# Gated delta rule in a streaming encoder: the powers and the inverse of the 16-token blocks kept as packed 32-column tiles

## The chip, the cores and the metric

The kernel runs on one core of one Trainium2 chip. The metric is the device time of one execution in microseconds. The engines are TensorE (PE), VectorE (DVE), ScalarE (ACT), GpSimd (POOL) and SyncE (SP); they run side by side and wait for each other by semaphores only.

## What is computed

A two-layer encoder trunk over 256 tokens of width 2048, all in float32: a gated DeltaNet layer, then an S5 layer, each with its MLP and an input embedding. The change lies in the DeltaNet layer. It has 32 value heads and 16 key heads of 128, and it is computed in chunks of 64 tokens:

```python
m = jnp.where(strict, jnp.einsum('bhnid,bhnjd->bhnij', kb, k) * decay, 0.0)
t_inv = lax.linalg.triangular_solve(eye + m, jnp.broadcast_to(eye, m.shape),
                                    left_side=True, lower=True, unit_diagonal=True)
u = jnp.einsum('bhnij,bhnjd->bhnid', t_inv, v * beta[..., None])
w = jnp.einsum('bhnij,bhnjd->bhnid', t_inv, kb * jnp.exp(gc)[..., None])
...
v_new = u_n - jnp.einsum('bhck,bhkv->bhcv', w_n, state)
```

What matters here is t_inv, the inverse of a unit lower triangular 64x64 matrix for each chunk and head.

## The kernel before

Every large product streams its weights from HBM in chunks of 2048x128 numbers. ACT rounds a chunk to w_hi (L280), DVE computes the rest w_lo = raw - w_hi (L286), in four quarters of 128x512 each, and PE multiplies a quarter by four key tiles (L299 to L303). One order of the work is written out by hand for each engine; nothing is scheduled by a planner.

The DeltaNet layer has 16 rounds (`head(r)` on PE, ACT and DVE), one for each key head with its two value heads. A round has 24 steps. In each step PE multiplies one quarter of the streamed projection weights, which belong to the next heads, and then does one part of the delta rule (`core(r, s)`), so that the products fill the time in which a part waits for ACT and DVE. ACT and DVE have the same two kinds of work in their queues: the splits of the weights (`low(s)` on DVE) and the parts.

The four matrices of a round (two value heads, two blocks of 128 tokens, so two chunks on the diagonal of each) lie side by side as [128, 4, 128] in one tile. The inverse is built from the inside. `key_matrix` (L1796) forms Mp, the matrix m, and keeps in Pm minus its part within blocks of 16 tokens. The inverse of such a block is (I + P)(I + P^2)(I + P^4)(I + P^8). RT holds the transposed inverse so far, starting as P^T + I (L1811). DVE's transpose turns blocks of 32x32 on the spot, which turns these block-diagonal matrices completely. The steps of the change are:

- step 0: PE squares P into bank C (`four`, L633, four products of 128x128 with 128 columns each), ACT copies it to P2.
- step 1: PE multiplies P2 by RT into bank A; DVE adds it to RT (`add_to_R`, L1838). DVE turns P2 into P2T (L1842), PE multiplies P2T by P2 for the fourth power, ACT copies it to P4.
- step 2: the same with P4 and P4T (L1847), giving P8; PE also does the products of q and k (L656).
- step 3: PE multiplies P8 by RT, DVE adds; PE turns k (L663).
- steps 4 to 9: the blocks of 16 are joined to 32, 64 and the chunk, with products of Mp, RT and Dm, the transpose of RT (L667 to L701). The first, L667, waits for the third `add_to_R`.

The order of DVE's queue around it is fixed in `head`: after `key_matrix(r + 1)` come mid_lo (L1922), `low(22)`, `low(23)`, and in the next round `low(0)`, the transpose of P2, `low(1)`, the first addition, `low(2)`, the transpose of P4, a convolution (`conv`, L1769 to L1775), the second addition, the masked products of q and k with `low(3)` between them (L1854, L1857), the third addition, and the transpose of RT (L1860). P2, P8, WT and the output tile oy share the tile T[0]; therefore ACT waits for mid_lo of the round before in step 0.

## Time and profile before

| | |
|---|---|
| median of 3 runs | 3187.47 us (3186.65 to 3192.27) |
| span of the profiled execution | 3188.2 us (its own run time is not listed apart from the three) |
| PE busy | 3099.4 us, 97% |
| DVE busy | 2246.8 us, 70% |
| ACT busy | 1742.8 us, 55% |
| POOL busy | 821.5 us, 26% |
| HBM traffic | 556.43 MB, 175 GB/s over the span |

The 16 rounds of the DeltaNet layer lie between about 87 and 899 us of the span; the rest is the output projection, the MLPs and the S5 layer. Busy times of the engines overlap. A line number points to the instruction's source line, and for helpers (L286 is `split_lo`, L941 is ACT's `A_`) to the helper. Matmuls are pipelined: an instruction's end lies later than the start of the next.

### The profile page before, as it was taken

What the parts mean: (1) busy time and instruction counts of PE and PEld (TensorE: products, weight loads), DVE (VectorE), ACT (ScalarE), POOL (GpSimd) and SP (SyncE); (2) the same over time, 40 slices, a digit from 0 to 9 for tenths busy, and PEclk for the clock granted to TensorE, in tenths of its full rate; (3) what the DMA queues carried; (4) which work ended last, traced back from release to release, by engine and by line L of the source; (5) the groups of instructions that cost most, each with busy time, mean ns of one, the idle gap of its engine ahead of it and who ended that gap; (6) DMA issues with size and microseconds to landing.
All of it is one profiled execution on the core that took longest, in us unless ns stands there. A gap on an engine that the chain in (4) does not pass through costs nothing.

```text
span 3188.2 us, 63691 instructions
## 1 busy us (share of the span) xinstructions
PE 3099.4 (97%) x19926; PEld 2737.0 (86%) x19926; DVE 2246.8 (70%) x4157; ACT 1742.8 (55%) x3855; POOL 821.5 (26%) x1372
## 2 busy tenths in 40 slices
PE   5999999999999999999999999999999999999998
PEld 4999999999978888888888887888888888888887
DVE  5767777777755788667887767886677654776566
ACT  5565666566644555445555556764555544555444
POOL 1000000000010499888888810770000000000000
PEclk8999999999999999999999999999999999999999
DMA  6454444444467777877777766785666677667764
GB/s 166 115 135 123 125 122 132 128 125 122 132 170 190 195 204 208 226 203 203 202 206 208 211 183 166 231 247 153 185 182 186 189 185 185 183 185 185 185 159 142
DMA packets 1036179, 556.43 MB, mean 175 GB/s; under 512 B 38193, under 2 KB 1023953, under 8 KB 1035585
## 3 DMA queue, kind: packets, MB, share of 16 engines
q1 hardware_dynamic: 969088, 491.18, 57.8%
q10 hardware_dynamic: 58160, 37.63, 4.0%
q0 software_dynamic: 8848, 26.59, 2.7%
q8 instruction: 44, 0.72, 0.1%
q14 instruction: 39, 0.31, 0.0%
HBM read 528.30 MB, written 27.03 MB: 174 GB/s over the span
## 4 chain that ended last, share of the span: by engine, by line
PE 73%; DVE 11%; ACT 7%; issue 6%; DMA 1%; ACTq 1%; DVEq 0%; POOL 0%; SPq 0%; POOLq 0%
PE bank L302 39%; PE bank L303 21%; DVE w_lo L286 5%; ACT w_hi L280 3%; PE bank L633 2%; PE bank L299 1%; ACT T L941 1%; PE bank L300 1%; DVE tiles L1935 1%; ACT L941 1%; DVE normed L1947 1%; DVE tiles L328 1%; PE bank L798 1%; ACT dec L941 1%; DVE y L1775 1%
## 5 line engine op out<-in xcount | busy, mean ns | idle before, releaser
L286 DVE TENSOR_TENSOR w_lo<-raw,w_hi 128x512 fp32r<-128x512 f32 x1856 | 1298.1, 752 | 145.2 <-ACT w_hi L280 137.3
L302 PE MATMUL bank<-act,w_hi 128*128 128x512 f32 x3376 | 1227.5, 405 | 17.5 <-DVE w_lo L286 7.8
L303 PE MATMUL bank<-act,w_lo 128*128 128x256 f32 x4352 | 1224.3, 281 | 0.0
L302 PE MATMUL bank<-mid,w_hi 128*128 128x512 f32 x3072 | 1088.1, 399 | 4.1 <-DVE w_lo L286 3.1
L280 ACT ACTIVATE w_hi<-raw 128x512 fp32r<-128x512 f32 x1856 | 1040.9, 620 | 68.7 <-PE bank L303 44.1
L303 PE MATMUL bank<-mid,w_lo 128*128 128x256 f32 x3072 | 860.7, 280 | 0.0
L303 PEld LDWEIGHTS bank<-act,w_lo 128*128 128x128 f32 x4352 | 827.9, 190 | 0.8
L302 PEld LDWEIGHTS bank<-act,w_hi 128*128 128x128 f32 x3376 | 638.1, 189 | 171.9 <-DVE w_lo L286 11.2
L302 PEld LDWEIGHTS bank<-mid,w_hi 128*128 128x128 f32 x3072 | 579.1, 188 | 147.0 <-issue 3.4
L303 PEld LDWEIGHTS bank<-mid,w_lo 128*128 128x128 f32 x3072 | 581.6, 189 | 0.2 <-issue 0.2
L318 ACT ACTIVATE tiles<-bank 128x256 f32<-128x256 f32 x323 | 123.5, 382 | 541.8 <-PE bank L303 535.6
L328 DVE TENSOR_TENSOR tiles<-bank,tiles 128x256 f32<-128x256 f32 x288 | 121.4, 421 | 357.0 <-ACT tiles L318 349.3
L299 PE MATMUL bank<-act,w_hi 128*128 128x256 f32 x976 | 296.1, 303 | 0.0
L300 PE MATMUL bank<-act,w_hi 128*128 128x256 f32 x976 | 276.1, 283 | 0.0
L1436 POOL DMA_DIRECT2D chunk_no<-in_constants_dram x1 | 0.5, 548 | 828.4 <-DVE mid L1922 828.4
L299 PEld LDWEIGHTS bank<-act,w_hi 128*128 128x128 f32 x976 | 186.8, 191 | 5.5 <-issue 3.6
L300 PEld LDWEIGHTS bank<-act,w_hi 128*128 128x128 f32 x976 | 187.2, 192 | 4.5 <-issue 4.1
L941 ACT ACTIVATE mid<-normed 128x256 f32 (+1 forms) x128 | 53.5, 418 | 247.6 <-DVE normed L1947 247.6
L941 ACT ACTIVATE T<-bank 128x512 f32<-128x512 f32 (+2 forms) x144 | 68.8, 478 | 204.2 <-PE bank L633 75.4
L1949 DVE TENSOR_TENSOR mid<-normed,mid 128x256 f32 (+1 forms) x128 | 59.1, 462 | 94.3 <-ACT mid L941 94.3
L338 ACT ACTIVATE sqb<-h 128x256 f32 (+1 forms) x96 | 40.1, 418 | 130.6 <-DVE h L1979 62.3
L1775 DVE SCALAR_TENSOR_TENSOR y<-pre,conv_f,y 128x256 f32<-128x256 f32 x192 | 93.1, 485 | 6.8
(331 smaller groups left out, 3122.6 us busy)
## 6 DMA issues: line engine op xcount, KB each, us to landing
raw<-in_mlp_w_up_dram SPq DMA_DIRECT2D x128, 1024.0 KB, 6.6
raw<-in_mlp_w_down_dram SPq DMA_DIRECT2D x128, 1024.0 KB, 6.2
raw<-in_gdn_w_in_dram SPq DMA_DIRECT2D x96, 1024.0 KB, 6.0
raw<-in_gdn_w_out_dram SPq DMA_DIRECT2D x32, 1024.0 KB, 6.8
raw<-in_ple_w_gate_dram SPq DMA_DIRECT2D x32, 1024.0 KB, 6.3
raw<-in_s_w_out_dram SPq DMA_DIRECT2D x28, 1024.0 KB, 6.8
raw<-in_s_w_in_dram ACTq DMA_DIRECT2D x10, 1024.0 KB, 7.1
c_scratch<-c_pow ACTq DMA_DIRECT2D x32, 256.0 KB, 4.6
```

The lines of the kernel that those rows point to most:

```text
L280: eng.activation(w_hi[par][:, c], raw[slot][:, c], ACT.Copy).then_inc(S("hi_ready"), 1)
L286: eng.tensor_tensor(w_lo[par][:, c], raw[slot][:, c], w_hi[par][:, c].bitcast(F32), ALU.subtract).then_inc(S("lo_ready"), 1)
L299: eng.matmul(a[:, 0:NT], w_hi[par][:, w], rhs[:, k0 + kt, 0:NT], start=(k0 + kt == 0), stop=False)
L300: eng.matmul(a[:, 0:NT], w_hi[par][:, w], rhs[:, k0 + kt, NT:2 * NT], start=False, stop=False)
L302: eng.matmul(a[:, :], w_hi[par][:, w], rhs[:, k0 + kt, :], start=(k0 + kt == 0), stop=False)
L303: mm = eng.matmul(a[:, 0:NT], w_lo[par][:, w], rhs[:, k0 + kt, 0:NT], start=False, stop=(k0 + kt == kend - 1))
L318: eng.activation(half[:, par, :], acc[par][:, NT:2 * NT], ACT.Copy).then_inc(S("half_copied"), 1)
L328: eng.tensor_tensor(dst, acc[par][:, 0:NT], half[:, par, :], ALU.add).then_inc(S("acc_freed"), 1)
L633: mm = pe.matmul(bk[:, m * P:(m + 1) * P], lhs[:, m, :], rhs[:, m, :], start=True, stop=True)
L941: return se.activation(dst, src, f, **kw)
L1775: ins = STT(y[:, j, :], pre[:, j, k:k + NT], conv_f[:, j, k:k + 1], y[:, j, :], ALU.mult, ALU.add)
L1949: TT(mid[:, span(i * 4 + j, 1), NT:2 * NT], normed[:, a, :], mid[:, span(i * 4 + j, 1), 0:NT].bitcast(F32), ALU.subtract).then_inc(S("hidd ...
```

## The change

The diagonal blocks of 32x32 hold all that is not zero, so four matrices of 128x128 fit into 32 columns each. The new tile pr is [128, 4, 2, 32]: for each matrix the packed transposed power (index 0) and the packed transposed inverse (index 1). Two tiles px[0], px[1] hold the power spread out again as a block-diagonal 128x128 matrix, as a stationary operand; their other blocks are cleared once at the start by POOL. `four` multiplies px (in step 0 Pm itself) by 32 or 64 columns of pr: with 64 the one product gives the next power and the inverse's update together. Step 0 has 32 columns, steps 1 and 2 have 64, step 3 has 32.

On DVE, `key_matrix` turns Pm by four transposes, one for each 32 partitions, into pr, and adds a packed identity. `spread(i, src)` writes the four blocks of a power into px by four transposes; the first two read ACT's copy, the third reads bank C directly. `add_to_R` works on the packed halves. The convolution comes after the third spread and the second addition. The last update of the inverse is written into RT, block by block, by four additions.

RT's other blocks must be zero now when they are read (ACT fills some of them later in a round, as before), so POOL clears three regions of RT in each round once the key products are done, and DVE's last additions wait for that (`RT_cleared`). ACT makes two copies of 128x128 instead of three of 128x512, and its wait for mid_lo moves from step 0 to step 4, since only WT is left in T[0] there.

```diff
@@ -158,16 +158,22 @@
         gcr = gs("gcr", [P, 4, P])
+        pr = gs("pr", [P, 4, 2, 32])
+        px = [gs(f"px{i}", [P, 4, P]) for i in range(2)]
+        ident32 = gs("ident32", [P, 32])
         g1.close()
+
+        block_32 = lambda t_, j: t_[32 * j:32 * j + 32, :, 32 * j:32 * j + 32]
+        pair_of = lambda bk, i: bk[:, 0:256].rearrange("p (m i q) -> p m i q", m=4, i=2)[:, :, i, :]
...
-        P2, P8, WT, osq, oy = (T[0],) * 5
-        rn, Pm, P4, Dm = (T[1],) * 4
-        sq, PT, P4T = (T[2],) * 3
-        P2T, VN, orn = (T[3],) * 3
+        WT, osq, oy = (T[0],) * 3
+        rn, Pm, Dm = (T[1],) * 3
+        sq = T[2]
+        VN, orn = (T[3],) * 2
@@ -625,12 +631,10 @@
-            def four(bk, lhs, rhs, name, turn_=False):
+            def four(bk, power, first, count, name):
                 for m in range(4):
-                    if turn_:
-                        mm = pe.transpose(bk[:, m * P:(m + 1) * P], lhs[:, m, :], ident)
-                    else:
-                        mm = pe.matmul(bk[:, m * P:(m + 1) * P], lhs[:, m, :], rhs[:, m, :], start=True, stop=True)
+                    mm = pe.matmul(bk[:, m * 64:m * 64 + 32 * count], power[:, m, :],
+                                   pr[:, m, first:first + count, :].rearrange("p i q -> p (i q)"), start=True, stop=True)
                 mm.then_inc(S(name), 1)
@@ -638,27 +642,25 @@
                     w("PT_ready")
-                    four(C, PT, Pm, "power_done")
+                    four(C, Pm, 0, 1, "power_done")
                 elif s == 1:
-                    w("power_out", 3, 1)
                     w("RT_ready", 7, 1)
-                    four(A, P2, RT, "R_done")
-                    w("transposed_out", 2, 1)
-                    four(C, P2T, P2, "power_done")
+                    w("power_out", 2, 1)
+                    w("spread_out", 3, 1)
+                    four(A, px[0], 0, 2, "power_done")
                 elif s == 2:
-                    w("power_out", 3, 2)
                     w("RT_ready", 7, 2)
-                    four(A, P4, RT, "R_done")
-                    w("transposed_out", 2, 2)
-                    four(C, P4T, P4, "power_done")
+                    w("power_out", 2, 2)
+                    w("spread_out", 3, 2)
+                    four(C, px[1], 0, 2, "power_done")
                     w("o_normed")
...
                 elif s == 3:
-                    w("power_out", 3, 3)
                     w("RT_ready", 7, 3)
-                    four(A, P8, RT, "R_done")
+                    w("spread_out", 3, 3)
+                    four(A, px[0], 1, 1, "R_done")
                     w("o_log")
@@ -1081,25 +1083,23 @@
                 if s == 0:
-                    w("mid_lo")
+                    w("RT_ready", 7, 1)
                     w("power_done", 3, 1)
-                    A_(fl(P2), C[:, :]).then_inc(S("power_out"), 1)
+                    A_(pr[:, :, 0, :], pair_of(C, 0)).then_inc(S("power_out"), 1)
                 elif s == 1:
                     w("power_done", 3, 2)
-                    A_(fl(P4), C[:, :]).then_inc(S("power_out"), 1)
-                elif s == 2:
-                    w("power_done", 3, 3)
-                    A_(fl(P8), C[:, :]).then_inc(S("power_out"), 1)
+                    A_(pr[:, :, 0, :], pair_of(A, 0)).then_inc(S("power_out"), 1)
                 elif s == 3:
...
                 elif s == 4:
+                    w("mid_lo")
                     w("X_done", 3, 1)
...
                 elif s == 5:
-                    w("R_done", 6, 4)
+                    w("R_done", 4, 2)
                     for j in range(4):
@@ -1107,7 +1107,7 @@
                 elif s == 7:
-                    w("R_done", 6, 5)
+                    w("R_done", 4, 3)
                     for j in range(2):
@@ -1119,7 +1119,7 @@
                 elif s == 9:
-                    w("R_done", 6, 6)
+                    w("R_done", 4, 4)
                     A_(RT[0:64, :, 64:128], C[0:64, 0:256].rearrange("p (m q) -> p m q", m=4), scale=-1.0).then_inc(S("RT_ready"), 1)
@@ -1425,11 +1425,20 @@
                 gp.dma_start(dst, src, allow_slow_non_contiguous=dst.shape[-1] == 1).then_inc(S("side_in"), 16)
+            for t_ in px:
+                gp.memset(t_[:, :, :].rearrange("p m q -> p (m q)"), 0.0).then_inc(S("px_cleared"), 1)
+            gp.memset(RT[:, :, :].rearrange("p m q -> p (m q)"), 0.0).then_inc(S("RT_cleared"), 1)
             gp.wait_ge(S("gc_turned_out"), 1)
...
             gp.dma_start(gcr[:, :, :].rearrange("p (b h) q -> p b (h q)", b=2), gc_rows(0)).then_inc(S("gc_saved"), 16)
+            with gp.Fori(1, KH) as r:
+                gp.wait_ge(S("kk_done"), r + 1)
+                gp.sem_inc(S("RT_read"), 1)
+                gp.memset(RT[0:32, :, 32:64], 0.0).then_inc(S("RT_cleared"), 1)
+                gp.memset(RT[64:96, :, 96:128], 0.0).then_inc(S("RT_cleared"), 1)
+                gp.memset(RT[0:64, :, 64:128], 0.0).then_inc(S("RT_cleared"), 1)
             gp.wait_ge(S("t_in"), 16)
@@ -1749,6 +1758,7 @@
             link(ve.memset(pre[:, :, 0:4], 0.0))
+            link(ve.memset(WT[96:128, :, :].rearrange("p m q -> p (m q)"), 0.0))
@@ -1806,10 +1816,17 @@
                 ve.wait_ge(S("P_ready"), r + 1)
-                ve.transpose(fl(PT), fl(Pm)).then_inc(S("PT_ready"), 1)
+                for j in range(4):
+                    last = ve.transpose(pr[32 * j:32 * j + 32, :, 0, :], block_32(Pm, j))
+                last.then_inc(S("PT_ready"), 1)
                 ve.wait_ge(S("PT_ready"), r + 1)
-                TT(RT[:, :, :], PT[:, :, :], ident.unsqueeze(1).to_broadcast([P, 4, P]), ALU.add).then_inc(S("RT_ready"), 1)
-
+                TT(pr[:, :, 1, :], pr[:, :, 0, :], ident32[:, :].unsqueeze(1).to_broadcast([P, 4, 32]),
+                   ALU.add).then_inc(S("RT_ready"), 1)
+
+            link(TT(ident32[:, :], ident[:, 0:32], ident[:, 32:64], ALU.add))
+            link(TT(ident32[:, :], ident32[:, :], ident[:, 64:96], ALU.add))
+            link(TT(ident32[:, :], ident32[:, :], ident[:, 96:128], ALU.add))
+            ve.wait_ge(S("px_cleared"), 2)
             scalars(0)
@@ -1832,21 +1849,28 @@
-                def add_to_R(i):
-                    w("R_done", 6, i)
+                def spread(i, src):
+                    if i < 3:
+                        w("power_out", 2, i)
+                    else:
+                        w("power_done", 3, 3)
+                    for j in range(4):
+                        last = ve.transpose(block_32(px[(i + 1) % 2], j), src[32 * j:32 * j + 32])
+                    last.then_inc(S("spread_out"), 1)
+
+                def add_to_R(i, bk):
                     w("RT_ready", 7, i)
-                    TT(fl(RT), A[:, :], fl(RT), ALU.add).then_inc(S("RT_ready"), 1)
+                    TT(pr[:, :, 1, :], pair_of(bk, 1), pr[:, :, 1, :], ALU.add).then_inc(S("RT_ready"), 1)
                 low(0)
-                w("power_out", 3, 1)
-                ve.transpose(fl(P2T), fl(P2)).then_inc(S("transposed_out"), 1)
+                spread(1, pr[:, :, 0, :])
                 low(1)
-                add_to_R(1)
+                spread(2, pr[:, :, 0, :])
+                add_to_R(1, A)
                 low(2)
-                w("power_out", 3, 2)
-                ve.transpose(fl(P4T), fl(P4)).then_inc(S("transposed_out"), 1)
+                spread(3, pair_of(C, 0))
+                add_to_R(2, C)
                 conv(r, n + 2, 2)
-                add_to_R(2)
@@ -1855,7 +1879,12 @@
                 TT(qkT[:, :, :], qkT[:, :, :], U.unsqueeze(1).to_broadcast([P, 4, P]), ALU.mult).then_inc(S("qkT_ready"), 1)
-                add_to_R(3)
+                w("R_done", 4, 1)
+                w("RT_ready", 7, 3)
+                w("RT_cleared", 3, 1)
+                for j in range(4):
+                    whole = TT(block_32(RT, j), pair_of(A, 0)[32 * j:32 * j + 32], pr[32 * j:32 * j + 32, :, 1, :], ALU.add)
+                whole.then_inc(S("RT_ready"), 1)
                 w("RT_ready", 7, 4)
```

On DVE, at the start of a round's part (transposes and additions between the weights' splits). Before, up to the first addition to the inverse:

```order
L1842 STREAM_TRANSPOSE T<-T 128x512 [waits power_out]
L284 REGISTER_ALU
L286 TENSOR_TENSOR w_lo<-raw,w_hi 128x512 [waits hi_ready]
L1829 REGISTER_ALU
L1829 ISA [waits R_done]
L1838 TENSOR_TENSOR RT<-bank,RT 128x512 [waits RT_ready]
L284 REGISTER_ALU
L286 TENSOR_TENSOR w_lo<-raw,w_hi 128x512 [waits hi_ready]
```

Now, from the first spread on; px is the spread-out power, pr the packed tile:

```order
L1858 STREAM_TRANSPOSE px<-pr 32x4x32 [waits power_out]
L1858 STREAM_TRANSPOSE px<-pr 32x4x32 x3
L290 REGISTER_ALU
L292 TENSOR_TENSOR w_lo<-raw,w_hi 128x512 [waits hi_ready]
L1846 REGISTER_ALU
L1858 STREAM_TRANSPOSE px<-pr 32x4x32 [waits power_out]
L1858 STREAM_TRANSPOSE px<-pr 32x4x32 x3
L1846 ISA
L1863 TENSOR_TENSOR pr<-bank,pr 128x4x32 [waits RT_ready]
L290 REGISTER_ALU
L292 TENSOR_TENSOR w_lo<-raw,w_hi 128x512 [waits hi_ready]
```

The one transpose of the whole tile became four of 32 partitions, the second spread comes ahead of the first addition, and between the two spreads lies one split.

On DVE, in front of the first product that joins blocks (L667). Before, from the product of q and k to the transpose of RT:

```order
L1854 TENSOR_TENSOR qkT<-dec,bank 128x512 [waits qk_done]
L284 REGISTER_ALU
L286 TENSOR_TENSOR w_lo<-raw,w_hi 128x512 [waits hi_ready]
L1857 TENSOR_TENSOR qkT<-qkT,masks 128x512 [waits qk_decay]
L1829 REGISTER_ALU [waits R_done]
L1838 TENSOR_TENSOR RT<-bank,RT 128x512 [waits RT_ready]
L1829 REGISTER_ALU
L1860 STREAM_TRANSPOSE T<-RT 128x512 [waits RT_ready]
```

Now:

```order
L1878 TENSOR_TENSOR qkT<-dec,bank 128x512 [waits qk_done]
L290 REGISTER_ALU
L292 TENSOR_TENSOR w_lo<-raw,w_hi 128x512 [waits hi_ready]
L1881 TENSOR_TENSOR qkT<-qkT,masks 128x512 [waits qk_decay]
L1846 REGISTER_ALU
L1846 REGISTER_ALU [waits R_done]
L1846 REGISTER_ALU [waits RT_ready]
L1886 TENSOR_TENSOR RT<-bank,pr 32x4x32 [waits RT_cleared]
L1886 TENSOR_TENSOR RT<-bank,pr 32x4x32 x3
L1846 REGISTER_ALU
```

The last addition is four instructions, with a wait for POOL's clears. The convolution, which stood between the second transpose and the second addition, now stands between the second addition and this place.

## Rows read from the trace of the kernel before

**Rows 1.** Page, first part: busy time, share of the span, instructions.
```profile
PE 3099.4 (97%) x19926; PEld 2737.0 (86%) x19926; DVE 2246.8 (70%) x4157; ACT 1742.8 (55%) x3855; POOL 821.5 (26%) x1372
```

**Rows 2.** Windows, one round; columns: us, busy of each engine (instructions), PEclk, DMA.
```profile
433.36:485.13 51.77, 51.25 (x397) 47.71 (x397) 38.38 (x78) 32.70 (x74) 0.00 (x0) 1.00 0.48 127
```

**Rows 3.** Waits of PE, rounds between 122.72 and 847.49: waiter, releaser, total, times, longest.
```profile
PE bank L633 <- DVE T L1842: 3.3, 14, 0.2
PE bank L633 <- DVE T L1809: 2.7, 14, 0.2
```

**Rows 4.** Chain of waits through one round: start us, us, what.
```profile
433.36 1.17 ACT dec L941 x4
...
442.56 0.69 DVE qkn L1793
...
452.17 1.16 PE bank L633 x8
...
476.16 0.46 PE bank L712 x4
```

**Rows 5.** Timeline of DVE in that round: start us, us, instruction, [idle before <-releaser].
```profile
447.64 0.71 DVE L1809 STREAM_TRANSPOSE T<-T 128x512 f32<-128x512 f32 x1
448.39 0.69 DVE L1811 TENSOR_TENSOR RT<-T,consts 128x512 f32<-128x512 f32 x1
449.00 0.69 DVE L1922 TENSOR_TENSOR mid<-T,mid 128x512 f32 x1
449.60 1.89 DVE L286 TENSOR_TENSOR w_lo<-raw,w_hi 128x512 fp32r<-128x512 f32 x3
451.41 0.71 DVE L1842 STREAM_TRANSPOSE T<-T 128x512 f32<-128x512 f32 x1
...
454.63 0.13 DVE L1769 COPY conv_f<-conv_w 128x4 f32 x1
...
456.62 0.68 DVE L1838 TENSOR_TENSOR RT<-bank,RT 128x512 f32<-128x512 f32 x1
457.22 0.68 DVE L1854 TENSOR_TENSOR qkT<-dec,bank 128x512 f32<-128x512 f32 x1
...
459.38 0.69 DVE L1838 TENSOR_TENSOR RT<-bank,RT 128x512 f32<-128x512 f32 x1 [0.28 <-PE bank L633]
...
461.65 0.42 DVE L328 TENSOR_TENSOR z<-bank,tiles 128x256 f32<-128x256 f32 x1
461.98 0.41 DVE L1781 SCALAR_TENSOR_TENSOR y<-tiles,y 128x256 f32<-128x256 f32 x1
```

**Rows 6.** Timeline of PE in the same stretch.
```profile
448.50 1.13 PE L633 MATMUL bank<-T 128*128 128x128 f32 x8 [0.20 <-DVE T L1809]
...
450.88 1.05 PE L633 MATMUL bank<-RT,T 128*128 128x128 f32 x8
452.17 1.16 PE L633 MATMUL bank<-T 128*128 128x128 f32 x8 [0.23 <-DVE T L1842]
...
454.58 1.05 PE L633 MATMUL bank<-RT,T 128*128 128x128 f32 x8
455.47 1.06 PE L633 MATMUL bank<-T 128*128 128x128 f32 x8
...
460.60 0.91 PE L667 MATMUL bank<-RT,Mp 128*112 128x64 f32 x8
```

**Rows 7.** Timeline of DVE, its only small transpose of the round.
```profile
468.56 0.30 DVE L1876 STREAM_TRANSPOSE T<-RT 32x128 f32<-32x128 f32 x1 [1.05 <-ACT RT L941]
```

**Rows 8.** Timeline of ACT: two runs of four instructions, two copies out of PSUM.
```profile
433.26 1.27 ACT L941 ACTIVATE dec<-gcr,hs 128x128 f32<-128x128 f32 x4
...
453.36 0.60 ACT L941 ACTIVATE T<-bank 128x512 f32<-128x512 f32 x1 [2.44 <-PE bank L633]
...
463.76 0.89 ACT L941 ACTIVATE RT<-bank 16x64 f32<-16x64 f32 x4 [1.31 <-PE bank L673]
...
476.64 0.38 ACT L941 ACTIVATE state<-bank 128x256 f32<-128x256 f32 x1 [0.66 <-PE bank L712]
```

## The prediction

> **What bounds the kernel now.** I read the page first. TensorE (PE) is busy for 97% of the span [rows 1], so the change, which takes matmul columns away, seems to aim at the right engine. But a busy PE says nothing about one stage, so I went to the stage that the change touches, the rounds of the delta rule. They repeat exactly: a round takes 51.77 us, with PE busy for 51.25, VectorE (DVE) for 38.38, ScalarE (ACT) for 32.70, GpSimd (POOL) for nothing, at a granted clock of 1.00 [rows 2]. Next the waits of PE over the 14 middle rounds: only two sorts, both of 0.2 us a round, and both at the very products of the change, for DVE's transposes at L1809 and L1842 [rows 3]. That is the warning. The chain of waits says why: in a round it runs over ACT at 433.36, over DVE from 442.56, over PE only from 452.17 to 476.16, and then over ACT and DVE again [rows 4]. A round is thus a ring that is PE's for half its length. The first powers lie on the DVE half, and PE looks full there because it multiplies streamed weights while DVE works.
>
> The DVE instructions of this half follow each other without a gap: 447.64, 448.39, 449.00, 449.60 (three w_lo tiles), 451.41 [rows 5]. PE starts its second power at 452.17, when the transpose of 451.41 (0.71 long) ends, and did the inverse's product at 450.88 while it waited [rows 5, 6].
>
> **What the change does to PE.** Six groups of four products of 128 columns become four groups of 32 or 64 columns. A group now costs 0.89 (454.58 to 455.47) [rows 6]. The nearest row to the new ones, four products of 64 columns with 112-wide weights, starts at 460.60 and lasts 0.91 against 1.05 for a 128-column group [rows 6]. So a new group ends about 0.95 after it starts and holds PE for some 0.79; from nothing saved (0.89) to columns alone (0.22 for 32 columns) are the ends. I take 0.79: PE's own work falls by 6 x 0.89 - 4 x 0.79 = 2.2 us a round. That is worth something only where PE ends last.
>
> **What it does to DVE.** One transpose of 128x512 becomes four of 32x128, each on another 32 partitions, and that four times a round (the first power, three spreads) where there were three. The last addition becomes four instructions too. Three additions shrink to 128x128. The prices:
> - A small transpose: the only one in the trace lasts 0.30 alone [rows 7]. A 128x512 one lasts 0.71, and fills the four groups of partitions at once [rows 5]. Two ends for four small ones: if each waits for the one before, 4 x 0.30 = 1.20; if they overlap as whole-width neighbours do (128x512 additions last 0.68 and start every 0.60, 128x256 ones last 0.42 and start every 0.33 [rows 5], so 128 elements start every 0.20), 3 x 0.20 + 0.30 = 0.90. The floor is one whole transpose, 0.71.
> - Which end? ACT does both kinds in this round. Four 128x128 instructions on all partitions take 1.27 together, though one lasts 0.39 on average, so they overlap. Four of 16x64, each on other partitions, take 0.89, and one lasts 0.215: four times 0.215 is 0.86, so nothing overlaps [rows 8]. I take the first end, 1.20, for DVE too. The Trainium skill says this of DVE itself (VectorE: DVE Perf Modes, the section on two Vector instructions with no wait between them): an instruction that starts in another group of 32 partitions than the last one is held until every earlier one has finished. By that rule the group is 1.20. No DVE row here has such neighbours, so no row confirms it.
> - A small addition lasts 0.29 (0.42 less half of 0.68 - 0.42): four on different partitions 1.16, or 0.89 if they overlap. On all partitions a 128x128 one takes 0.20 instead of 0.60.
>
> **The new path**, on the clock of this round, from the first transpose at 447.64:
> 1. Four transposes into the packed tile, 1.20 and 0.04 to the next: 448.88 (before 448.39). The identity's addition 0.20 for 0.61; mid 0.60, three w_lo 1.80: DVE is free at 451.48 (before 451.41). The copy of the packed power was ready long before: PE from about 449, 0.95, and a 128x128 copy of 0.27 on ACT (0.60 for 512 elements, 0.38 for 256 [rows 8]).
> 2. Spread 1, 1.20: PE's next group starts at 452.73. PE has been ready since 448.95 + 0.79 + 1.49 (a quarter, 448.50 to 450.88 less 0.89 [rows 6]) = 451.2. The inverse's product that filled this hole is merged into the late one: 1.5 us of PE lie open.
> 3. The merged product after a stall: 1.0; copy 0.27 and 0.06 of handing over; spread 2 from 454.06 to 455.26. The next merged product reads the inverse's half too, so it also waits for the first packed addition, 0.29 behind the spread: PE at 455.60 (its old pair began at 454.58). DVE was free from 453.3 on, after one w_lo: a new wait of 0.7.
> 4. Product 1.0; DVE does a w_lo meanwhile; spread 3 reads the bank from 456.63 to 457.83.
> 5. Only now comes the convolution, which used to start at 454.63: addition 0.20, convolution 1.99 (454.63 to 456.62), masked q k 0.60, w_lo 0.60, mask 0.60 (456.62 to 457.22 is one such step) [rows 5]: 461.82. Before, DVE had these behind it early enough to start the last addition at 459.38, after a wait of 0.28 for PE.
> 6. Four final additions 1.16 and handing over 0.06: PE starts L667 at 463.05 instead of 460.60 [rows 6].
>
> So PE, which had saved 2.2 us of work, stands still for 2.5 us in front of L667 (from its second pair at 455.47 to L667 it now takes 5.13, two groups included [rows 6]; 455.60 + 5.13 - 2 x 0.10 = 460.5), and the round is longer by **2.45 us**. From L667 to 476.16 PE ends last as before: DVE is later than PE by another half microsecond there, but had waits of its own. Nothing later is shortened, since the rest of the ring is untouched. The part is run once per pair of heads, 16 times: 16 x 2.45 = 39.2 us.
>
> **Costed at nothing.** ACT's three copies shrink by 0.3 each and lose the third; ACT waits for PE in front of them, and stands on the ring elsewhere. ACT's wait for mid_lo moves to a place four steps later, long after the signal. Its tanh is queued behind the convolution, 3 us later than now, and the four instructions behind the tanh, the copy of L667's result last, are ACT steps of at most 0.60 each: from 460.0 they are through by about 462, before L667 even starts, so that copy is not late. POOL's three clears are released by the key products, 15 us before the additions need them, and POOL is empty; if they got in DVE's way, I put it at one small instruction, 0.30 a round. The opening's four extra DVE instructions (about 1 us) lie in front of a stretch where DVE waits for ACT's w_hi; without that cover they cost 1 us once.
>
> The profiled span is 3188.2 us, 0.7 above the median of 3187.47; no time of its own is given for that execution, so I put the sum on the median: 3187.5 + 39.2 = **3227 us**.
>
> **The rivals.**
> - **Small instructions overlap**, 0.90 and 0.89 a group. Five groups lie on the path, so 2.45 - 4 x 0.30 - 0.27 = 1.0 a round: 3203. Speaks for it: DVE's whole-width neighbours overlap. Against: ACT's do not across partitions. The Trainium skill (Vector Engine (DVE) Microarchitecture Reference, measured stream behaviour) gives some 75 ns per instruction beside 1.04 ns per element; that makes an estimated 0.21 each, 0.83 a group, near this case.
> - **A group costs no more than the whole transpose did**, 0.71, by four groups of partitions at work together: 2.45 - 5 x 0.47 = 0.1 a round, 3189, no change. No row shows two DVE instructions in full overlap.
> - **PE ends last after all, and the kernel is faster.** With no stall PE would go from 448.50 to L667 in 12.1 - 6 x 0.89 - 0.4 of stalls + 4 x 0.79 = 9.5 us, 2.6 less: 16 x 2.6 = 42, 3146. The place is the queue between 451.41 and 459.38. It decides only if DVE has its final additions done by 458.0, which is 5.0 us sooner than my path; even the overlapping case finds only 1.5 of them. Partial gains lie between.
> - **More than I count**: a gap behind each held instruction (0.05 x 20 = 1 us a round, 3243), or a clock that falls. Before, PE never stands for more than 0.2 us in a round and the clock is 1.00; now it would stand for 1.5 and 2.5. If it fell to the lower level for one quarter, about 1.4 us more a round: 3249.
>
> **How the numbers follow.** Forecast 0.60, overlap 0.15, no change 0.08, faster 0.08, more than counted 0.09. The likeliest gives 3227. Leaving out the two cases below and the far end of the last one, the range is 3196 to 3246. A measurement of this kernel can tell about 0.2%, 6.4 us. Slower by more than that: 0.60 + 0.09 and most of the overlap case, 0.82; within it 0.09; faster 0.09.
>
> **What would show it.** In the profile after: rounds of about 54.2 us; PE waiting some 1.5 us a round at its second power group for the DVE spread, and over 2 us at the successor of L667 for the final additions; four transposes in about 1.2; the convolution more than 3 us later in the round; PE busy share lower, with no drop of the clock. I am wrong in the price if four small ones take 0.9, and wrong in the mechanism if PE waits nowhere between the first power and that product, or if the round is shorter than 51.6.

## The result, and the profile after

The changed kernel takes 3248.9 us (median of 4 runs, 3241.98 to 3263.9), the kernel before in the same comparison 3187.99 us. The ratio is 1.0201, with a 95% interval of 1.0172 to 1.023: the change costs 2%, 61 us. The forecast had the direction (slower, 0.82) and the place; its 3227 us is 22 us short, and the time lies 2.9 us above the range. The profiled execution is the slowest of the four, 3263.9 us with a span of 3262.2.

The page, parts 1 and 5 (busy time, share of the span, instructions; and GpSimd's new row):

```profile
PE 3097.8 (95%) x19670; PEld 2719.3 (83%) x19670; DVE 2287.7 (70%) x4417; ACT 1721.9 (53%) x3839; POOL 822.6 (25%) x1420
...
L1439 POOL MEMSET RT<- 32x128 f32 x15 | 2.9, 194 | 840.4 <-PE bank L608 840.4
```

TensorE's busy time fell by 1.6 us in all [rows 1], although 256 matmul instructions are gone. DVE has 260 instructions more and 41 us more work. The clears by POOL are 0.19 us each and nobody waits for them.

The rounds are measured between DVE's first instructions on Mp. The windows of the first round, of a stretch of the second, and of two neighbouring rounds in the middle; columns: us, busy of each engine (instructions), PEclk, DMA share, GB/s:

```profile
83.62:141.90 58.28, 53.27 (x371) 48.78 (x370) 39.21 (x91) 29.79 (x69) 0.70 (x3) 0.91 0.42 116
159.90:168.00 8.10, 8.04 (x39) 7.43 (x39) 6.11 (x14) 2.70 (x8) 0.00 (x0) 0.59 0.44 121
423.34:479.98 56.64, 51.60 (x381) 47.13 (x380) 40.90 (x95) 31.46 (x73) 0.70 (x3) 0.97 0.44 116
479.98:535.10 55.12, 50.06 (x381) 45.75 (x380) 40.67 (x95) 31.47 (x73) 0.70 (x3) 1.00 0.45 119
```

Two things lie here on top of each other. A round at a granted clock of 1.00 takes 55.08 us on average against 51.77 [rows 2], 3.31 more. PE's busy time in it fell by 1.2 us while the round grew by 3.3, so PE now stands still for 5 us of each. And six of the 15 rounds are longer still: the first three at 58.1 to 58.3 us with a clock of 0.91 to 0.94, and three later ones at 56.65 with 0.97. In the stretch at 0.59 the engine ran mostly at the lower of its two levels, 1.2 GHz; it had stood for 2.24 us just before.

The waits of PE, 14 rounds between 132 and 920 us:

```profile
PE bank L669 <- DVE RT L1886: 31.4, 14, 2.2
PE bank L636 <- DVE px L1858: 17.9, 14, 1.3
PE bank L636 <- DVE pr L1820: 10.4, 14, 0.7
PE bank L636 <- DVE pr L1863: 9.7, 14, 0.7
```

Where there were two waits of 0.2 us a round [rows 3] there are four, of 2.2, 1.3, 0.7 and 0.7 us, together 5.0 us (69.4 / 14), and all are for DVE. The chain of waits through the same half of a round at clock 1.00 (start us, us, what) runs on DVE, with PE as short steps in between, where before it was PE's from the second power on [rows 4]:

```profile
538.38 1.06 PE bank L636 x8
...
541.82 0.32 DVE px L1858
542.18 1.12 PE bank L636 x8
...
544.91 0.30 DVE pr L1863
545.43 1.11 PE bank L636 x8
...
550.12 0.68 DVE qkT L1878
551.32 0.69 DVE qkT L1881
552.81 0.31 DVE RT L1886
553.16 1.00 PE bank L669 x8
```

DVE's timeline of this stretch answers to [rows 5]; columns: start, us, instruction, and in brackets the idle time before it with its releaser:

```profile
536.98 1.25 DVE L1820 STREAM_TRANSPOSE pr<-T 32x128 f32<-32x128 f32 x4
538.26 0.29 DVE L1823 TENSOR_TENSOR pr<-pr,ident 128x128 f32<-128x128 f32 x1
...
540.88 1.24 DVE L1858 STREAM_TRANSPOSE px<-pr 32x128 f32<-32x128 f32 x4
542.15 0.69 DVE L292 TENSOR_TENSOR w_lo<-raw,w_hi 128x512 fp32r<-128x512 f32 x1
543.63 1.25 DVE L1858 STREAM_TRANSPOSE px<-pr 32x128 f32<-32x128 f32 x4 [0.78 <-ACT pr L943]
544.91 0.29 DVE L1863 TENSOR_TENSOR pr<-bank,pr 128x128 f32<-128x128 f32 x1
545.12 0.68 DVE L292 TENSOR_TENSOR w_lo<-raw,w_hi 128x512 fp32r<-128x512 f32 x1
546.57 1.29 DVE L1858 STREAM_TRANSPOSE px<-bank 32x128 f32<-32x128 f32 x4 [0.76 <-PE bank L636]
...
551.92 1.18 DVE L1886 TENSOR_TENSOR RT<-bank,pr 32x128 f32<-32x128 f32 x4
```

A group of four transposes lasts 1.25 us, 0.31 for each, where one whole transpose lasted 0.71; the four last additions last 1.18. The group holds DVE for 1.27 us (540.88 to 542.15). A whole transpose, ahead of an instruction that does not wait for it, held DVE for 0.62 us, from 451.41 [rows 5] to this line of the kernel before:

```profile
452.03 0.65 DVE L286 TENSOR_TENSOR w_lo<-raw,w_hi 128x512 fp32r<-128x512 f32 x1
```

DVE also idles twice now, 0.78 us for ACT's copy and 0.76 for PE's bank, because DVE, PE and ACT hand one small result round in a ring.

PE's timeline in the same stretch:

```profile
539.26 0.48 PE L308 MATMUL bank<-act,w_hi 128*128 128x512 f32 x1
...
542.18 1.10 PE L636 MATMUL bank<-pr,px 128*128 128x64 f32 x8 [1.28 <-DVE px L1858]
543.09 0.48 PE L308 MATMUL bank<-act,w_hi 128*128 128x512 f32 x1
...
545.43 1.10 PE L636 MATMUL bank<-pr,px 128*128 128x64 f32 x8 [0.68 <-DVE pr L1863]
...
553.16 1.00 PE L669 MATMUL bank<-RT,Mp 128*112 128x64 f32 x8 [2.24 <-DVE RT L1886]
```

The timeline of the weight loads (PEld), after:

```profile
542.18 0.97 PEld L636 LDWEIGHTS bank<-pr,px 128*128 128x128 f32 x8 [1.60 <-DVE px L1858]
```

The same view of the kernel before:

```profile
454.46 0.97 PEld L633 LDWEIGHTS bank<-RT,T 128*128 128x128 f32 x8
...
460.48 0.88 PEld L667 LDWEIGHTS bank<-RT,Mp 128*112 128x112 f32 x8
```

And PE's next instruction behind that L667 group, in the kernel before:

```profile
461.31 0.48 PE L302 MATMUL bank<-act,w_hi 128*128 128x512 f32 x1
```

The groups with 32 columns begin at 538.38 and 548.31 and the next instruction of PE at 539.26 and 549.22: 0.88 and 0.91. A group with 64 columns takes 542.18 to 543.09, 0.91. With 128 columns it was 0.89 [rows 6]. The number of columns makes no difference from 32 to 128, and the eight weight loads of a group take 0.97 us either way. What does count is how wide the weights are. The L667 group has 64 columns too, but weights of 112 columns instead of 128: its loads take 0.88 us, and PE goes on 0.71 us after its start (460.60 [rows 6] to 461.31). The Trainium skill (TensorE: Matmul & The Clock Gate, the section on LDWEIGHTS) has that rule: the load goes by the columns of the stationary operand. Its figure of columns / 1.2 ns gives an estimated 8 x 107 ns = 0.85 us for a group, and the 0.88 to 0.91 us from a group to the next instruction agree within 0.06.

### The profile page after: what moved, and what is told of

Same layout as the page of the kernel before. It is cut to its first block, busy times and chain, and to the rows that moved or that the text cites. A ratio compares the mean times of both kernels' runs of the same rounds, so it can differ in the third digit from the quotient of the medians.

```text
span 3262.2 us, 63592 instructions
## 1 busy us (share of the span) xinstructions
PE 3097.8 (95%) x19670; PEld 2719.3 (83%) x19670; DVE 2287.7 (70%) x4417; ACT 1721.9 (53%) x3839; POOL 822.6 (25%) x1420
## 4 chain that ended last, share of the span: by engine, by line
PE 65%; DVE 16%; ACT 9%; issue 7%; DMA 2%; ACTq 1%; DVEq 1%; POOL 0%; SPq 0%; POOLq 0%
PE bank L308 35%; PE bank L309 19%; DVE w_lo L292 5%; ACT w_hi L286 3%; PE bank L636 2%; DVE px L1858 1%; PE bank L305 1%; ACT T L943 1%; PE bank L306 1%; DVE y L1785 1%; DVE tiles L334 1%; DVE tiles L1964 1%; DVE normed L1976 1%; ACT L943 1%; ACT uf L943 1%
## 5 line engine op out<-in xcount | busy, mean ns | idle before, releaser
L308 PE MATMUL bank<-act,w_hi 128*128 128x512 f32 x3376 | 1235.7, 408 | 20.1 <-DVE w_lo L292 8.8
L308 PE MATMUL bank<-mid,w_hi 128*128 128x512 f32 x3072 | 1091.1, 400 | 5.5 <-DVE w_lo L292 4.5
L308 PEld LDWEIGHTS bank<-act,w_hi 128*128 128x128 f32 x3376 | 643.3, 191 | 175.4 <-DVE w_lo L292 14.3
L308 PEld LDWEIGHTS bank<-mid,w_hi 128*128 128x128 f32 x3072 | 578.8, 188 | 150.3 <-DVE w_lo L292 4.1
L943 ACT ACTIVATE T<-bank 112x256 f32<-112x256 f32 (+2 forms) x96 | 40.1, 417 | 128.8 <-PE bank L726 44.9
```

The lines of the kernel that those rows point to most:

```text
L308: eng.matmul(a[:, :], w_hi[par][:, w], rhs[:, k0 + kt, :], start=(k0 + kt == 0), stop=False)
L943: return se.activation(dst, src, f, **kw)
```

## The experiments

Theory: the end of this half of a round is set by DVE's queue, made longer by (a) four instructions for one, (b) a convolution of 2 us in front of the last update, and (c) the handing round between engines; on top of it the stall of 2.24 us ahead of L669 lets the clock fall in some rounds. Rivals: the cost lies in the new waits themselves wherever DVE's work stands; small instructions are dear by their number and not by their partitions; the clock has nothing to do with the stall. Each comparison has its own runs of the kernel before: e1 to e4 one chip (before: 3186.62 us), e5 to e8 another (3186.21), the last four a third (3187.33).

**e1_conv_early**: the convolution back in front of the third spread.

```diff
                 low(2)
+                conv(r, n + 2, 2)
                 spread(3, pair_of(C, 0))
                 add_to_R(2, C)
-                conv(r, n + 2, 2)
```

> Only the order on DVE is changed: the convolution goes back in front of the third spread, where DVE waits 0.76 us a round for PE. Theory A (DVE's queue sets the end of the round's first half, and PE waits for its last additions): the 0.76 us are filled, PE waits 0.8 us less in front of the first joining product, an undisturbed round takes 54.3 us instead of 55.1, and the time falls by 12 us, to about 3237. Theory B (the chain power, copy, spread, product sets it): the third spread and the fourth product group come over 1 us later, and the round takes 55.5 us or more.

3233.21 us (3221.57 to 3239.03, 4 runs), ratio 1.0146 (1.0109 to 1.0182). Rounds 54.22 us, all at clock 1.00. The wait ahead of L669 fell from 2.2 us to 0.2, but the one for the second packed addition (L1863) rose to 1.1: the convolution now holds up the third spread. So its place costs 0.86 us of the 3.31, not the 2 us that it lasts.

**e2_both_filled**: in addition `low(2)` goes ahead of the second spread, into the time in which DVE waits for ACT.

```diff
                 low(1)
+                low(2)
                 spread(2, pr[:, :, 0, :])
                 add_to_R(1, A)
-                low(2)
+                conv(r, n + 2, 2)
                 spread(3, pair_of(C, 0))
                 add_to_R(2, C)
-                conv(r, n + 2, 2)
```

> Order on DVE again: the third w_lo quarter goes in front of the second spread (DVE waits 0.78 us there) and the convolution in front of the third. Theory A: both waits are filled, nearly 1.5 us leave the path, an undisturbed round takes 53.6 us, the time is about 3225, still slower than before by 1%. Theory B: 55 us or more a round.

3220.77 us (3202.8 to 3225.4, 4 runs), ratio 1.0105 (1.0059 to 1.015), rounds 53.63 at clock 1.00, as worked out. Both orders together are worth 1.45 us a round, and 1.86 remain.

**e3_same_group**: the four transposes of a spread all read the first 32 partitions of a tile of zeros and write to the first 32 of px. Their number, size and waits stay; only the change of partitions is gone. The powers above the first so become zero and drop out of the inverse.

```diff
+        zt = gs("zt", [P, 4, 32])
...
                     for j in range(4):
-                        last = ve.transpose(block_32(px[(i + 1) % 2], j), src[32 * j:32 * j + 32])
+                        last = ve.transpose(px[(i + 1) % 2][0:32, :, 32 * j:32 * j + 32], zt[0:32])
```

> The four transposes of each spread all lie on the first 32 partitions and turn a tile of zeros, so the higher powers drop out of the inverse; the instructions have the same shape and number. If the price of four small instructions comes from changing the group of partitions, a group takes about 0.95 us instead of 1.25, and an undisturbed round 54.1 us. If it comes from the number of instructions alone, a group stays at 1.25 and a round at 55.1.

DVE's timeline in this kernel, a changing and an unchanging group:

```profile
358.62 1.25 DVE L1822 STREAM_TRANSPOSE pr<-T 32x128 f32<-32x128 f32 x4
...
362.52 0.87 DVE L1860 STREAM_TRANSPOSE px<-zt 32x128 f32<-32x128 f32 x4
```

Four transposes on one group of partitions take 0.87 us, four on changing groups 1.25, in one execution and with the same shapes. So without the change they do overlap, close to the 0.90 us that the prediction had put as its lower end. Counted to the start of an instruction that waits for none of them, it is 0.81 us (362.52 to 363.33) against 1.27 in the changed kernel and 0.62 for a whole transpose. Of the 0.65 us by which a group of four holds DVE longer than one whole transpose, 0.46 are the change of partitions and 0.19 the number. The small ones of e3 read another tile than the real ones; that this has no part in it was not tested. The Trainium skill (VectorE: DVE Perf Modes, the section on two Vector instructions with no wait between them) says that an instruction that starts in another group of 32 partitions is held until the earlier ones have finished, and this pair of rows agrees. Undisturbed rounds are 53.64 us, 1.4 less than with the real spreads (3 x 0.46 = 1.4). The whole kernel took 3237.05 us (2 runs, ratio 1.017, 1.0129 to 1.021) all the same, because nine of its 15 rounds ran at 0.97, and the first at 0.94: the stall ahead of L670 (L669 in the changed kernel) is still 1.8 us. That is a first sign for the clock.

**e4_fill**: nine products into an unused part of a bank ahead of PE's wait in step 4. They compute nothing that is read.

```diff
                 elif s == 4:
+                    for _ in range(9):
+                        pe.matmul(C[:, 2 * P:3 * P], kq[:, 1, 0, :], kq[:, 1, 0, :], start=True, stop=True)
                     w("RT_ready", 7, 4)
```

> Nine products of 128 columns whose result nobody reads are added on PE in front of its wait for the last additions, where it stands still for 2.2 us; they take 2.0 us and end before that wait does. If the rounds of 56.6 and 58.1 us come from TensorE's clock falling after that stall, every round now takes 55.1 us, the clock reads 1.00 and the time falls by 10 to 14 us although PE has more to do. If the clock has nothing to do with the stall, the time stays at 3249 with a mean clock of 0.985.

3245.96 us (3241.99 to 3248.99, 4 runs), ratio 1.0194 (1.0162 to 1.0226). Every round is 55.05 to 55.13 us at clock 1.00 (only the first at 0.97), but the median is not clearly below 3248.9. So both kernels were run again on one chip.

**a_again** and **e4_again**: the changed kernel, and the filled one, unchanged.

> The changed kernel unchanged, beside the filled one on one chip. Theory that the stall of 2.24 us ahead of the group that uses RT lets the clock fall in some rounds: about 3249 us, mean clock about 0.985 to 0.99, undisturbed rounds of 55.1 us with some of 56.6 to 58.3 us among them. Rival, that the 14 us of the first profile were a mishap of one execution: all rounds 55.1 us, clock 0.99 or more, about 3240 us.

> The nine filler products ahead of TensorE's wait again, on the chip that runs the changed kernel too. Theory of the clock: every round 55.1 us at 1.00, and 8 to 14 us less than the changed kernel in this comparison. Rival, that the clock costs nothing in most executions: the same time as the changed kernel within 3 us.

3251.95 us (3243.29 to 3259.54, 6 runs) and 3241.58 us (3233.59 to 3247.55, 6 runs); ratios 1.0218 (1.0188 to 1.0248) and 1.0186 (1.0158 to 1.0215), which overlap by a little. Windows of 600 us in the middle, the changed kernel and then the filled one:

```profile
300.00:900.00 600.00, 544.51 (x4094) 497.68 (x4093) 442.15 (x1012) 338.61 (x774) 7.75 (x33) 0.99 0.44 117
```

```profile
300.00:900.00 600.00, 566.65 (x4322) 520.24 (x4321) 444.88 (x1020) 340.48 (x786) 7.73 (x33) 1.00 0.45 119
```

In the changed kernel again five rounds of 15 ran at 0.94 to 0.97 and took 56.65 to 56.70 us, the others 55.05 to 55.13. In the filled one 14 of 15 are 55.05 to 55.11 us, all at 1.00, and the first is 53.97. Its 15 rounds sum to 824.9 us against 834.2. Work that nobody needs makes the kernel 9 us shorter in the rounds of the profiled executions and 10.4 us in the median. With the stall filled the clock stays up, so it is this stall that lets the clock fall. The rounds show it cleanly; the two ratios alone would not quite. Where the stall is at most 1.3 to 1.4 us (e1, e2) no round lost clock.

**e5_before_four**: the kernel before, with the transpose of P2 alone made of four small ones, into a cleared tile of its own.

```diff
+        P2T = gs("p2t", [P, 4, P])
...
-                ve.transpose(fl(P2T), fl(P2)).then_inc(S("transposed_out"), 1)
+                for j in range(4):
+                    last4 = ve.transpose(P2T[32 * j:32 * j + 32, :, 32 * j:32 * j + 32], P2[32 * j:32 * j + 32, :, 32 * j:32 * j + 32])
+                last4.then_inc(S("transposed_out"), 1)
```

> The kernel before, with one thing of the change: the transpose of P2 is four transposes of 32 partitions into a cleared tile of its own. It lies on the path (PE waits 0.23 us for it in every round). If four small instructions on changing groups of partitions run one after the other, they take 1.25 us for 0.71 and a round 52.3 us for 51.8, the time 3195. If they overlapped the round would grow by under 0.25 us.

3193.69 us (3189.53 to 3202.9, 8 runs), ratio 1.0031 (1.0012 to 1.0049). Rounds 52.31 us, 0.54 more. The four small transposes end 1.24 us after their start and the whole one after 0.71, so PE's product is released 0.53 us later; its wait for this transpose grew from 0.2 to 0.8. Here the half microsecond by which the transpose ends later is half a microsecond of the round.

**e6_masked**: the packed form, without small spreads. In e2's order DVE turns the packed power straight out of the bank by one instruction (32x32 blocks on all partitions) and multiplies it, repeated four times, by a mask of diagonal blocks into px. The last update is made the same way, so RT needs no clears by POOL. The two tiles px become one.

```diff
...
+                    ve.transpose(tp[:, :, :], pair_of(bk, 0)).then_inc(S("tp_ready"), 1)
+                    w("tp_ready", 3, i)
+                    by_block(px[(i + 1) % 2][:, :, :], tp[:, :, :]).then_inc(S("spread_out"), 1)
...
-                    whole = TT(block_32(RT, j), pair_of(A, 0)[32 * j:32 * j + 32], pr[32 * j:32 * j + 32, :, 1, :], ALU.add)
-                whole.then_inc(S("RT_ready"), 1)
+                TT(tp[:, :, :], pair_of(A, 0), pr[:, :, 1, :], ALU.add).then_inc(S("R_whole"), 1)
+                w("R_whole", 1, 1)
+                by_block(RT[:, :, :], tp[:, :, :]).then_inc(S("RT_ready"), 1)
```

> As both_filled, with whole-width instructions in the place of the groups of four: a spread is one transpose of the packed power straight out of the bank and one product with a block mask over 128x512, the last addition one packed addition and one such product; POOL clears nothing. Theory A: a spread takes 0.95 us instead of 1.28 and the last update 0.95 instead of 1.2, four places on the path, so an undisturbed round falls from 53.6 to about 52.4 us, the time to about 3198. Rival: the first power's latency holds the round, which stays above 53.

3200.07 us (3188.82 to 3206.34, 10 runs), ratio 1.0046 (1.0032 to 1.0061), rounds 52.33: 1.30 us a round less than e2. The mask product writes four times as much as is needed, and transpose and mask together (0.96 us, shown under e7) are cheaper than four exact instructions (1.27); and ACT's copy is no longer on the way to the spread. How the 1.30 us part between the two was not tested.

**e7_order**: e6 with DVE's queue in another order: the first spread ahead of `low(0)`, `low(2)` and `low(3)` ahead of the third with the convolution back behind it, and the two products of q and k (L1878, L1881) moved to behind `low(6)` and `low(7)`, where their result is still early enough.

```diff
-                low(0)
                 spread(1, C)
+                low(0)
                 low(1)
-                low(2)
                 spread(2, A)
-                conv(r, n + 2, 2)
+                low(2)
+                low(3)
                 spread(3, C)
+                conv(r, n + 2, 2)
...
                 gate(n + 3, 1, y[:, 3, :])
...
+                TT(bh(qkT), bh(dec), qk, ALU.mult).then_inc(S("qk_decay"), 1)
                 low(7)
...
+                TT(qkT[:, :, :], qkT[:, :, :], U.unsqueeze(1).to_broadcast([P, 4, P]), ALU.mult).then_inc(S("qkT_ready"), 1)
```

> As masked, and DVE's queue in another order: the first spread in front of the round's first w_lo quarter, two w_lo quarters in the wait before the third spread, the two masked q k instructions moved behind the joining of blocks, where DVE waits anyway. Theory A: DVE has the last update done when PE arrives, so PE sets the end here and its two spared product groups (1.8 us) count: a round of 50.8 to 51.2 us, the time 3172 to 3180, faster than before. Rival: the moved work makes DVE late in the second half, and the round stays at 51.8 or more.

3181.33 us (3177.43 to 3187.44, 11 runs), ratio 0.9984 (0.9975 to 0.9993): 0.16% faster than the kernel before, a little less than a measurement of this kernel can usually tell, with rounds of 51.31 us. DVE's timeline, a spread and the last update:

```profile
448.02 0.31 DVE L1858 STREAM_TRANSPOSE tp<-bank 128x128 f32<-128x128 f32 x1
448.37 0.69 DVE L1850 TENSOR_TENSOR px<-tp,bd 128x512 f32<-128x512 f32 x1
448.98 1.28 DVE L294 TENSOR_TENSOR w_lo<-raw,w_hi 128x512 fp32r<-128x512 f32 x2
...
456.07 0.29 DVE L1873 TENSOR_TENSOR tp<-bank,pr 128x128 f32<-128x128 f32 x1
456.39 0.69 DVE L1850 TENSOR_TENSOR RT<-tp,bd 128x512 f32<-128x512 f32 x1
```

A spread holds DVE for 0.96 us, to the start of its next instruction, and DVE idles nowhere in it.

**e8_before_order**: the same two moves in the kernel before, nothing packed: the transpose of P2 ahead of `low(0)`, the products of q and k behind `low(6)` and `low(7)`.

```diff
-                low(0)
                 w("power_out", 3, 1)
                 ve.transpose(fl(P2T), fl(P2)).then_inc(S("transposed_out"), 1)
+                low(0)
...
-                TT(bh(qkT), bh(dec), qk, ALU.mult).then_inc(S("qk_decay"), 1)
                 low(3)
...
-                TT(qkT[:, :, :], qkT[:, :, :], U.unsqueeze(1).to_broadcast([P, 4, P]), ALU.mult).then_inc(S("qkT_ready"), 1)
                 add_to_R(3)
...
                 gate(n + 3, 1, y[:, 3, :])
...
+                TT(bh(qkT), bh(dec), qk, ALU.mult).then_inc(S("qk_decay"), 1)
                 low(7)
...
+                TT(qkT[:, :, :], qkT[:, :, :], U.unsqueeze(1).to_broadcast([P, 4, P]), ALU.mult).then_inc(S("qkT_ready"), 1)
```

> The kernel before with DVE's order alone changed in the same way (P2's transpose in front of the first w_lo quarter, the masked q k instructions later), nothing packed. Before, PE ends last from the second power on and stands still for only 0.4 us in front of it, so at most 0.4 us a round are to be had: 51.4 us, the time 3181. If the order were all that makes the other version fast, both would be equal.

3174.57 us (3168.97 to 3179.09; one further execution took 7568.61 us at a mean granted clock of 0.46 and is no measure of the kernel), ratio 0.9964 (0.9945 to 0.9984): the lowest median of the study, though its interval overlaps that of e7. Rounds 51.26 us. PE's waits, rounds between 300 and 900 us:

```profile
PE bank L633 <- DVE T L1809: 2.2, 11, 0.2
```

Of the waits that come back in every round only the one for the first power is left, and PE is busy for 592.2 of these 600 us (579.6 in e7). In e7 packing has saved PE work, yet the round is no shorter (51.31), since the time lies in the ring. The moved lines are enough for all that e7 gains over the kernel before; packing adds nothing to them.

**e9_small_late**: e7's order with the change's own small transposes and additions.

```diff
-                low(0)
                 spread(1, pr[:, :, 0, :])
+                low(0)
                 low(1)
                 spread(2, pr[:, :, 0, :])
                 add_to_R(1, A)
                 low(2)
+                low(3)
                 spread(3, pair_of(C, 0))
...
```

> The small transposes of the change with the order that gave 3181 us with masked ones. Theory that VectorE's queue sets the end and that four small instructions cost 0.55 us more than one: rounds of 52.0 to 52.6 us, about 3192 to 3202 us. Rival, that the order alone made the gain and the form of the transposes is of no weight: rounds of 51.3 us, 3181 us.

3206.22 us (3195.82 to 3218.08, 10 runs), ratio 1.0065 (1.0044 to 1.0087): a little above what was expected. Rounds 52.67 us, all but the first (53.35, 0.97) at clock 1.00. PE's waits, 300 to 900 us:

```profile
PE bank L636 <- DVE px L1858: 8.2, 12, 0.8
PE bank L636 <- DVE pr L1820: 8.1, 11, 0.7
PE bank L636 <- DVE pr L1863: 8.1, 12, 0.7
PE bank L669 <- DVE RT L1880: 5.4, 12, 0.6
```

With this kernel the cost is parted: the order alone takes 2.41 us a round (55.08 to 52.67) and 46 us in all from the changed kernel, the drops of the clock among them; masked instead of small instructions, with ACT's copy off the path, take another 1.36 us a round (to 51.31) and 25 us (e7's median, from another chip).

**e10_order2**: e7 with the product for `low(3)` behind the last update.

```diff
                 low(2)
-                low(3)
                 spread(3, C)
...
+                low(3)
                 low(4)
```

> The masked, reordered kernel with the product for low(3) behind the last update. Theory of the queue: 0.25 us less per round, rounds of 51.05 us, about 3177 us. Rival, that another wait takes over: 51.3 us and 3181 us as before.

3181.67 us (3167.82 to 3192.87, 12 runs), ratio 0.9991 (0.9969 to 1.0013), rounds 51.31: nothing gained, the rival is right. DVE's timeline shows where it went:

```profile
451.69 0.29 DVE L1857 TENSOR_TENSOR pr<-bank,pr 128x128 f32<-128x128 f32 x1 [0.68 <-PE bank L638]
```

In the place of the 0.6 us split DVE waits 0.68 us for PE's product. From the first transposes to the successor of L667 it is 12.42 us in both kernels. The ring of DVE and PE is now bound by its own steps.

## Why the prediction was right in kind and short in size

On the clock of a round that starts with the first transposes (536.98 in the profile after), step by step:

| | predicted | measured |
|---|---|---|
| first spread starts | +3.84 | +3.90 |
| PE's second group | +5.09 | +5.20 |
| second spread | +6.42 | +6.65 |
| PE's third group | +7.96 | +8.45 |
| third spread | +8.99 | +9.59 |
| last additions | +14.18 | +14.94 |
| L669, successor of L667 | +15.41 | +16.18 |
| the same before | +12.96 | |

- **The mechanism stands.** DVE's queue takes PE's place, PE stands where it was said (1.3 us, 1.5 predicted, ahead of the second group; 2.24, 2.5 predicted, ahead of L669), the convolution starts 4.1 us later in the round (548.10 - 536.98 = 11.12; before 454.63 - 447.64 = 6.99), where over 3 were forecast, and behind L669 the round grew by only 0.09 us more, so ACT's tanh and POOL's clears cost no more than that together.
- **Small instructions on changing partitions do not overlap.** The end taken from ACT's small rows, 1.20, was right (1.25), and 1.16 for the additions too (1.18). The two rivals with overlap are out by these rows. Four transposes that stay on one group do overlap (0.87 in e3), but the change has none of these.
- **What failed is the term of 2.45 us a round: it measured 3.31.** At L669 it is 3.22, 0.77 more than predicted, and this is spread over the hops of the ring: from the second spread to PE's third group 0.26 (PE starts 0.23 us after the addition has ended, where 0.05 was put), the two products with their way to DVE 0.23 (1.10 long after a stall, not 1.0), four transposes of 1.25 to 1.29 for 1.20, and 0.16 in the queue from the third spread to the last additions. The rival "more than I count" had such a gap, priced at 1 us a round and 3243 us, with little chance.
- **The clock was put into that rival alone**, at 1.4 us in every round, and the forecast said "no drop of the clock". It does drop, by more in a round that is hit (1.57 to 3.2 us) and in fewer rounds (6 or 5 of 15).
- **The sum as it came out**: 16 x 3.31 = 53 us give 3240.5 on the median of before; the rounds at a lower clock add 8 us (second profile: 834.2 - 15 x 55.08) to 14 us (first profile, 840.2 - 826.2). That is 3248 to 3255, and the medians are 3248.9 and 3252.0. Neither miss alone would have left the range: 3227 + 16 x 0.86 is 3241, and 3227 + 8 to 14 is 3235 to 3241.
- **PE's groups were put at 0.79 and cost 0.88 to 0.91.** The row they were taken from has weights of 112 columns; the rows of the weight loads would have told. The 2.2 us of PE work said to be saved are 1.7 (6 x 0.89 less 4 x 0.90). It changed nothing, as PE does not end last; it did touch the rival in which the kernel becomes faster, which had reckoned with 0.79 as well. Its condition, DVE through with the last update 10.4 us after the first transposes (458.0), was not met even by e7: 12.4.

The executions also differ behind the rounds. From Mp of the last round to the end of the span it is 2338.4 and 2338.7 us in the two profiles of the changed kernel and 2328.3 in the kernel before, so 10 of the 74 us between the profiled spans of before and after lie there. It is 2326.2 us in e7 and 2338.4 in e10, although nearly all of that is the same code. Much of this goes with the clock again. In the 100 us behind that Mp the granted clock is 1.00 in e7 and 0.91 in e10, and the third addition to h of the next stage starts 71.66 us behind it in e7 (925.03) and 78.33 us in e10 (930.50): 6.7 of the 12 us. In the two profiles of the changed kernel the clock of these 100 us is 0.95 and 0.93, in the filled one 1.00, in the kernel before 0.98. Why it falls there in one execution and not in another, also where the stall ahead of L669's successor is gone (e10), stays open; no run was aimed at it. The single executions of one kernel spread as much (e10: 3167.82 to 3192.87 us).

## What to carry to other kernels

Fewer columns in a matmul saved nothing here, since the weight loads took longer; count groups and the width of their weights before you count columns. On DVE a transpose and a mask product over all partitions (0.96 us) beat four exact instructions on changing groups of partitions (1.27), and in a ring between two engines each small step costs its hand-over as well. Before making an almost full engine lighter, look at which engine's queue stands in front of its waits: here two moved pieces of DVE's work gave 0.4% where the repacking, put into the old order, cost 2%.

## What was not expected of the hardware

- The clock fell only in some of the rounds that have the same stall of 2.24 us: in six of 15 in one execution and in five of 15 in another, mostly every fourth. With stalls of 1.8 us (e3) ten of 15 rounds were hit, more than with 2.24, so the length of the stall alone does not set it. With at most 1.4 us, or with the stall filled, none but a first round was. What picks the rounds stays open.
- Such a round does its work at the lower level for a stretch behind the stall. The stall of the hit round that starts at 423.34 ends at 441.40; the windows of the changed kernel behind it read 0.99, then 0.50:

```profile
441.40:443.10 1.70, 1.70 (x13) 1.61 (x14) 1.67 (x4) 0.61 (x2) 0.00 (x0) 0.99 0.94 268
443.10:446.00 2.90, 2.90 (x14) 2.71 (x13) 2.76 (x8) 0.45 (x2) 0.00 (x0) 0.50 0.68 180
```

  In an earlier hit round the lower level is there at once. PE's timeline after, behind the wait of a round that was hit, where L308's products take 0.63 us instead of 0.40:

```profile
159.96 1.76 PE L669 MATMUL bank<-RT,Mp 128*112 128x64 f32 x8 [2.24 <-DVE RT L1886]
161.48 0.78 PE L308 MATMUL bank<-act,w_hi 128*128 128x512 f32 x1
...
162.26 0.63 PE L308 MATMUL bank<-act,w_hi 128*128 128x512 f32 x1
```

- Most of the price of small instructions on DVE lies in the change of partitions (0.46 of the 0.65 us by which four hold DVE longer than one whole transpose), the rest in their number (0.19).
